# Three ready-made u tiles a head instead of two, turned in halves of 1024 columns over three buffer pairs

## The chip, the cores and the metric

The kernel runs on one core of one Trainium2 chip, in one launch. The metric is the device time of the launch in microseconds (us); lower is better.

## The reference

One decoder layer on 512 tokens of width 2048, in float32:

```
P = rms(x) @ w_in                       # 2048 x 6144: q | k | v | B | C | xc, 1024 columns each
a = 8 heads of differential attention   # softmax(s1) - lam * softmax(s2), applied to v, then rms
c = B * causal_conv3(C * xc)
x = x + concat(a, c) @ w_out
h = rms(x);  for 8 PEER heads: scores of 2 x 128 keys, top 16 of 16 x 16 sums, softmax gates
x = x + sum over the chosen experts e of gelu(h . u[e]) * gate * v[e]      # u, v: 16384 x 2048
```

## The kernel before

**Order of the work.** Five stages follow each other. (1) The qkv stage multiplies h by the first 3072 columns of w_in, in 6 chunks of 512 columns. (2) The heads stage has 8 rounds; each does one attention head and one 128-column block of the short convolution (three products called conv 0, 1 and 2, their weights in six pieces of 8 x 128 x 128 a head). (3) The out stage multiplies by w_out in 4 chunks. (4) The sweep: for 384 of the 512 tokens the product with u is dense over all 128 tiles of u (128 experts each, 16 tiles a sweep, 8 sweeps); the first 128 tokens gather their u and v rows by index. (5) The dense stage multiplies gelu times gate by all of v for 256 tokens and gathers v rows for 128.

Each float32 operand of a matmul is split into a high and a low part: ACT copies the high part (`wc_hi`, `uT_hi`), DVE subtracts it to get the low part (`wc_lo`, `uT_lo`), and PE makes three matmuls (lines L1811 to L1813).

**Queues.** Each engine has an order written out by hand and stops at the first wait that isn't met: SP issues loads on the hardware queue q1, POOL issues stores, zeroing and indirect transfers on the software queue q0, ACT has q10. POOL also computes the inverse roots (L752).

**u tiles.** The sweep needs u transposed. An even tile c is loaded to `u_tile[0]` from u, and PE transposes it with 16 transposes (L2063), 8 after each half of the 48 matmuls of tile c-1; ACT and DVE then split it out of PSUM (L1124, L1654). Of the odd tiles the first 56 (`TURNED`) are ready-made: in stages 1 to 3 SP loads the 128 rows into `near_rows` or `far_rows` (L473), DVE transposes 32 x 32 blocks (L1302, four of 128x512 a tile) into `near_turned` or `far_turned`, and the tile is stored in `uT_all` in DRAM by four transfers, one for each quarter of the partitions (L459). In the sweep SP loads such a tile into `u_tile[1]` (L654) and ACT and DVE split it straight from there (L1119, L1649). `turned_before(tile)` says which tiles these are: odd and below 112.

**A head of stage 2.** Two such tiles are made in each of the first seven heads, in the near pair. SP waits for `wc_ready` of piece p and then loads the piece after next (L566, 512 KB); after pieces 2 and 5 it also loads the next rows (`next_rows`). DVE transposes one tile in two halves among the softmax steps of query blocks 0 to 2, and the other after `o_n` (L1455) and before `qk_n` (L1379). POOL stores the first before it makes the inverse root of `o_ss`, the second after that of `qk_ss`. At the start of the stage DVE makes `wc_lo` of piece 2 and only then the norm of q and k of head 0:

```
            keep_qkv(chunks - 1)
            turn_rows(NEAR, NEAR_HEADS, "qkv")
            split_wc(0, 2)
            ...
            norm_qk(0, 0)
            norm_qk(0, 1)
```

ACT's order in a head, from `split_wc(j, 5)` on, is `exps(3)`, `split_wc(j + 1, 0)`, `keep_aT(2)`, `b_sb`, `split_wc(j + 1, 1)`, `keep_aT(3)`; PE needs aT of block 3 for its last product with v (`apply_v(3)`, L1910).

Of the kernel before, what the change touches and what calls it, by code (L numbers as in the profile page):

```python
# [34 lines left out]
P = 128  # L35
SEQ = 512
D = 2048
# [39 lines left out]
KEPT_BY_POOL = 1 + 2 * (HEADS - 1)  # L77
# [4 lines left out]
TURNED = NEAR_TURNED + FAR_TURNED  # L82
ZERO_DMAS = 2 * HEADS
# [22 lines left out]
def turned_before(tile):  # L106

    return tile % 2 == 1 and tile < 2 * TURNED
# [33 lines left out]
def decoder_layer(nc, x, attn_norm_g, w_in, q_norm_g, k_norm_g, lambda_q1, lambda_k1, lambda_q2, lambda_k2,  # L142
                  subln_g, conv_w, w_out, ffn_norm_g, peer_w_q, peer_subkeys, peer_u, peer_v, out):
    ctx = ExitStack()
    with ctx:
# [111 lines left out]
        seg_turned = [nc.alloc_sbuf_tensor_at("near_turned", [P, QUADS, KT, QUAD], F32, offset=late + 8 * KB), far_turned]  # L257
        wo0_hi = nc.alloc_sbuf_tensor_at("wo0_hi", [P, QUARTER, CHUNK], F32R, offset=late)
# [81 lines left out]
        uT_rows = u_tile[1][:, :].rearrange("p (a k e) -> p k a e", a=QUADS, e=QUAD)  # L340
# [12 lines left out]
        head_mean = sem("head_mean")  # L353
        head_rstd = sem("head_rstd")
# [17 lines left out]
        conv_gated = sem("conv_gated")  # L372
        conv_out = sem("conv_out")
# [43 lines left out]
        seg_kept = sem("seg_kept")  # L417
# [34 lines left out]
        def kept_at(pair, n):  # L452
            return n + pair * NEAR_TURNED

        def store_turned(engine, pair, n, stored):

            rows = uT_all[bass.ds(kept_at(pair, n) * P, P), :].rearrange("(r d) (a m) -> a d r m", r=QUADS, a=QUADS)
            for a in range(QUADS):
                engine.dma_start(rows[a], seg_turned[pair][QUAD * a:QUAD * (a + 1), :, :, :].rearrange("d r k e -> d r (k e)"))\  # L459
                    .then_inc(stored, 16)  # L460


        @nc_block.sync
        def _(sp):
# [7 lines left out]
            def load_rows(pair, n):  # L472
                sp.dma_start(seg_rows[pair][:, :], u_table[bass.ds((2 * kept_at(pair, n) + 1) * P, P), :])\  # L473
                    .then_inc(seg_in[pair], 16)

            def next_rows(pair, n):

                sp.wait_ge(seg_ready[pair], 4 * n + 4)
                load_rows(pair, n + 1)

            def keep_turned(pair, n, last=False):

                sp.wait_ge(seg_ready[pair], 4 * n + 4)
                if not last:
                    load_rows(pair, n + 1)
                store_turned(sp, pair, n, seg_stored[pair])
# [5 lines left out]
            def load_qkv_weights():  # L492

                def chunk(c, first=False):
                    load_wi(c, 0)
                    if first:
                        sp.wait_ge(hT_ps, TB)
                        load_rows(FAR, 0)
                    else:
                        keep_turned(FAR, 2 * c - 1)  # L500
                    load_wi(c, 1)
                    keep_turned(NEAR, 3 * c)
# [1649 lines left out]
```

## Time and profile before

| | us |
|---|---|
| median of 3 runs (2961.92 to 2970.81) | 2964.81 |
| the profiled execution's own time | 2968.59 |
| its span, first to last instruction | 2966.8 |
| qkv stage, heads stage, out stage and routing (about) | 45 to 288, 288 to 625, 625 to 860 |
| sweep, dense stage (about) | 860 to 2210, 2210 to 2960 |
| one head, PE's period | 40.9 |

In the windows view a line gives a stretch, its length, then for PE, the weight loads of PE (PEld), DVE, ACT and POOL the busy us and the count of instructions, the clock that PE was granted (1.00 is full speed), the mean busy share of the 16 DMA engines, and GB/s. In the timeline a line gives start us, length us, engine, line, operation, and in brackets how long the engine had been idle and what ended that. In a row of transfers the last number is the median us from issue to landing.

### The profile page before, as it was taken

To read this page: it belongs to the slowest core of one execution; us is meant where nothing else is said; L and a number is where in the kernel's file an instruction comes from. 1 tells how busy PE (TensorE), PEld (TensorE's weight loads), DVE (VectorE), ACT (ScalarE), POOL (GpSimd) and SP (SyncE) were. 2 spreads that over 40 slices of the span, in tenths; PEclk is the share of its full clock that TensorE was granted. 3 is DMA by queue.
4 is the path that set the end of the run, shared out by engine and by line. 5 is a ranking of instruction groups with operands and counts; after the bars stand their busy time and mean duration, and the time that the engine had idled before them with its cause. 6 is when DMAs were issued, how large, how long until landed. Compare 5 with 4: busy or idle time off the path is not lost.

```text
span 2966.8 us, 40581 instructions
## 1 busy us (share of the span) xinstructions
PE 2889.4 (97%) x14993; PEld 2570.9 (87%) x14993; DVE 2358.4 (79%) x3050; ACT 1048.8 (35%) x1373; POOL 1517.4 (51%) x906
## 2 busy tenths in 40 slices
PE   7999999999999999999999999999999999899898
PEld 6888777888889999999999999999998787777787
DVE  6455677754688888988888898899778898898898
ACT  4122443341323333434333343334233333333333
POOL 1000232300015656665665666566858887778662
PEclk9999999999999999999999999999999999999999
DMA  8998777779658998999899899999999999999998
GB/s 298 332 352 273 254 237 251 227 290 328 229 184 306 323 337 300 341 322 330 308 324 336 301 340 321 330 345 357 325 369 392 415 414 414 414 415 415 415 413 347
DMA packets 333295, 980.65 MB, mean 331 GB/s; under 512 B 63764, under 2 KB 180512, under 8 KB 241760
## 3 DMA queue, kind: packets, MB, share of 16 engines
q1 hardware_dynamic: 188560, 508.60, 46.7%
q0 software_dynamic: 107008, 439.75, 41.2%
q10 hardware_dynamic: 37584, 30.43, 3.2%
q8 instruction: 86, 1.41, 0.2%
q14 instruction: 57, 0.47, 0.0%
HBM read 866.33 MB, written 112.33 MB: 330 GB/s over the span
## 4 chain that ended last, share of the span: by engine, by line
PE 69%; DVE 10%; DMA 9%; issue 5%; POOL 4%; ACT 2%; SPq 0%; ACTq 0%; DVEq 0%; POOLq 0%
PE ps L1811 22%; PE ps L1813 21%; PE ps L1812 21%; DMA v_raw<-in_peer_v 7%; PE ps L2063 3%; DVE x_rows L1669 2%; DVE v_lo L1709 2%; DVE u_row L1660 2%; POOL gate_grid L820 1%; ACT v_hi L1180 1%; POOL dots L828 1%; POOL v_ring L839 1%; DMA gates_of<-gate_grid 1%; PE ps L1894 1%; PE ps L1910 1%
## 5 line engine op out<-in xcount | busy, mean ns | idle before, releaser
L1811 PE MATMUL ps<-hT_hi,uT_hi 128*128 128x384 f32 x2048 | 699.0, 341 | 10.3 <-DVE uT_lo L1649 6.1
L1813 PE MATMUL ps<-h2T_lo,uT_hi 128*128 128x384 f32 x2048 | 686.1, 335 | 0.0
L1812 PE MATMUL ps<-hT_hi,uT_lo 128*128 128x384 f32 x2048 | 685.0, 334 | 0.0
L820 POOL DMA_INDIRECT gate_grid<-gates,grid_cells x256 | 540.7, 2112 | 107.5 <-issue 78.8
L1811 PE MATMUL ps<-v_hi,a_hi 128*128 128x512 f32 x1024 | 404.2, 395 | 38.4 <-DVE v_lo L1709 37.7
L1180 ACT ACTIVATE v_hi<-v_raw 128x2048 fp32r<-128x2048 f32 x128 | 245.6, 1919 | 455.5 <-PE ps L1813 336.1
L1812 PE MATMUL ps<-v_hi,a_lo 128*128 128x512 f32 x1024 | 401.5, 392 | 0.0
L1813 PE MATMUL ps<-v_lo,a_hi 128*128 128x512 f32 x1024 | 401.2, 392 | 0.0
L1811 PEld LDWEIGHTS ps<-hT_hi,uT_hi 128*128 128x128 f32 x2048 | 384.8, 188 | 19.0 <-DVE uT_lo L1649 10.0
L1812 PEld LDWEIGHTS ps<-hT_hi,uT_lo 128*128 128x128 f32 x2048 | 385.0, 188 | 1.9
L1813 PEld LDWEIGHTS ps<-h2T_lo,uT_hi 128*128 128x128 f32 x2048 | 384.3, 188 | 0.0
L839 POOL DMA_INDIRECT v_ring<-in_peer_v,experts x128 | 286.3, 2237 | 136.2 <-DVE x_one L1759 104.8
L1709 DVE TENSOR_TENSOR v_lo<-v_raw,v_hi 128x2048 fp32r<-128x2048 f32 x128 | 293.1, 2290 | 71.7 <-ACT v_hi L1180 67.8
L1759 DVE SCALAR_TENSOR_TENSOR x_one<-v_ring,acts,x_one 128x2048 f32<-128x2048 f32 x128 | 300.3, 2346 | 7.8 <-DMA v_ring<-in_peer_v,experts 5.0
L810 POOL DMA_INDIRECT v_row<-in_peer_v,experts x128 | 140.3, 1096 | 322.7 <-DVE x_rows L1669 273.3
L1669 DVE SCALAR_TENSOR_TENSOR x_rows<-v_row,acts,x_rows 128x2048 f32<-128x2048 f32 x128 | 300.0, 2344 | 1.4 <-issue 1.4
L1660 DVE CUSTOM_DVE_ANT_0 u_row<-u_row,h_rows 128x2048 f32<-128x2048 f32 x128 | 292.6, 2286 | 3.5 <-DMA u_row<-in_peer_u,experts 3.5
L828 POOL DMA_INDIRECT dots<-products_one,cells x128 | 264.9, 2070 | 42.7 <-issue 38.7
L1811 PEld LDWEIGHTS ps<-v_hi,a_hi 128*128 128x128 f32 x1024 | 194.1, 190 | 87.4 <-issue 35.0
L1124 ACT ACTIVATE uT_hi<-ps 128x1024 fp32r<-128x1024 f32 x144 | 148.0, 1028 | 311.4 <-PE ps L2063 287.2
L1654 DVE TENSOR_TENSOR uT_lo<-ps,uT_hi 128x1024 fp32r<-128x1024 f32 x144 | 176.1, 1223 | 101.9 <-ACT uT_hi L1124 99.3
L1811 PE MATMUL ps<-w_hi,hT_hi 128*128 128x512 f32 x624 | 244.1, 391 | 1.2 <-DVE wi_lo L1256 1.2
(207 smaller groups left out, 4970.8 us busy)
## 6 DMA issues: line engine op xcount, KB each, us to landing
v_raw<-in_peer_v SPq DMA_DIRECT2D x128, 1024.0 KB
u_tile<-in_peer_u SPq DMA_DIRECT2D x72, 1024.0 KB
u_tile<-uT_all SPq DMA_DIRECT2D x56, 1024.0 KB
near_rows<-in_peer_u SPq DMA_DIRECT2D x40, 1024.0 KB, 8.4
uT_all<-near_turned SPq DMA_DIRECT2D x100, 256.0 KB, 7.0
w_raw<-in_w_in SPq DMA_DIRECT2D x24, 1024.0 KB, 9.0
wc_raw<-in_w_in SPq DMA_DIRECT2D x48, 512.0 KB, 6.7
far_rows<-in_peer_u SPq DMA_DIRECT2D x16, 1024.0 KB, 9.2
```

Of the source, the lines that this page charges most:

```text
L820: pool.indirect_dma_start(out=gate_grid, out_offset=bass.IndirectOffsetOnAxis(ap=grid_cells[:, d, col:col + 1], axis=0), in_=gates[:, 2 + ...
L828: pool.indirect_dma_start(out=dots[:, s:s + 1], out_offset=None, in_=products_one, in_offset=bass.IndirectOffsetOnAxis(ap=cells[:, col:col ...
L839: pool.indirect_dma_start(out=v_ring[s % RING][:, :], out_offset=None, in_=v_table, in_offset=slot(1, h, s)).then_inc(v_in[s % RING], 16)
L1180: nc.scalar.activation(v_hi[b % 2][:, :], v_raw[b % RAW_RING][:, :], ACT.Copy).then_inc(v_hi_ready, 1)
L1654: v.tensor_tensor(uT_lo[half][:, :, :], ps_uT[half], uT_hi[half][:, :, :].bitcast(F32), ALU.subtract)\
L1660: v.tensor_tensor_reduce(out=u_row[c % 2][:, :], in0=u_row[c % 2][:, :], in1=h_rows[:, 0, :], scale=1.0, scalar=0.0, op0=ALU.mult, op1=ALU ...
L1669: v.scalar_tensor_tensor(out=x_rows[:, 0, :], in0=v_row[c % 2][:, :], scalar=acts0[:, b:b + 1], in1=x_rows[:, 0, :], op0=ALU.mult, op1=ALU ...
L1709: v.tensor_tensor(v_lo[b % 2][:, :], v_raw[b % RAW_RING][:, :], v_hi[b % 2][:, :].bitcast(F32), ALU.subtract).then_inc(v_lo_ready, 1)
L1759: v.scalar_tensor_tensor(out=x_one[:, :], in0=v_ring[s % RING][:, :], scalar=acts[:, s:s + 1], in1=x_one[:, :], op0=ALU.mult, op1=ALU.add) ...
L1811: mm(out, a_hi, b_hi, start=first, stop=False)
L1812: mm(out, a_lo, b_hi, start=False, stop=False)
L1813: return mm(out, a_hi, b_lo, start=False, stop=last)
```

## The change

A head of the first seven now makes three tiles: the two odd ones as before, and the tile at place 6 of the sweep of the same number (tiles 6, 22, ..., 102), so that 63 tiles are ready-made, 7 of them even. The two pairs of stage 2 become three pairs of half buffers: LEFT and RIGHT are the halves of the near pair, THIRD lies at 124 KB and 140 KB of the arena, where `wi_lo` and `far_turned` lie in the qkv stage. Every half tile (128 rows x 1024 columns) is loaded by one 512 KB transfer with rows of 4 KB, transposed by two DVE instructions, and stored by four POOL transfers in runs of 1 KB (before: 1 MB with rows of 8 KB, four instructions, runs of 2 KB). DVE's six places in a head are: after `alibi` and `conv_taps`; after `combined(0)`; after `combined(1)`; after `combined(3)`; and two after `o_n`. SP loads half 0 after piece 1, halves 1 and 2 after piece 2, halves 3, 4 and 5 after pieces 3, 4 and 5. Before the loop of heads SP waits for the end of the qkv matmuls (`proj_done`), because THIRD lies over a buffer that they read; pieces 2 and later of head 0 are behind this wait. In the sweep tile 8 of each of the first seven sweeps is loaded when DVE has split tile 6, not when PE has turned it. Five semaphores are merged into others.

```diff
-KEPT_BY_POOL = 1 + 2 * (HEADS - 1)
+EXTRA = HEADS - 1
+EXTRA_AT = 6
+KEPT_BY_POOL = 1 + 3 * (HEADS - 1)
...
 def turned_before(tile):
 
-    return tile % 2 == 1 and tile < 2 * TURNED
+    if tile % TOPK == EXTRA_AT:
+        return tile // TOPK < EXTRA
+    return tile % 2 == 1 and tile < 2 * ODD_TURNED
...
+        half_rows.append(at("half_rows2", 124, [P, D // HALVES]))
...
+        half_turned.append(at("half_turned2", 140, [P, QUADS, KT // HALVES, QUAD]))
...
+        def half_place(j, i):
+
+            place = extra(j) if i >= 4 else odd_of_head(j, 1 + i // 2)
+            return place, i % 2
+
+        def half_of_head(i):
+
+            return (THIRD, LEFT, RIGHT)[i % 3]
+
+        def halves_turned(j, i):
+
+            return 4 * (NEAR_HEADS + 1) + 2 * (6 * j + i)
...
+            def next_half(j, i):
+
+                (tile, _), half = half_place(j, i)
+                sp.wait_ge(seg_ready[NEAR], halves_turned(j, i) - 4)
+                load_half(half_of_head(i), tile, half)
...
-            for n in range(2):
-                keep_turned(NEAR, NEAR_QKV + n)
+            keep_turned(NEAR, NEAR_QKV, odd(NEAR, NEAR_QKV), odd(NEAR, NEAR_QKV + 1))
+            sp.wait_ge(seg_ready[NEAR], 4 * NEAR_HEADS)
+            for x in (LEFT, RIGHT):
+                load_half(x, odd_of_head(0, 0)[0], x)
+            store_turned(sp, NEAR, odd(NEAR, NEAR_QKV + 1)[1], seg_stored[NEAR])
+            for t in range(TB):
+                sp.wait_ge(proj_done[t], QKV_CHUNKS)
             with sp.Fori(0, CT - 1) as j:
                 for p in range(PIECES):
                     sp.wait_ge(wc_ready, PIECES * j + p + 1)
                     conv_piece(j + (p + 2) // PIECES, (p + 2) % PIECES)
-                    if p in (2, 5):
-                        next_rows(NEAR, 2 * j + (NEAR_HEADS + p // 5))
+                    for i in ((), (0,), (1, 2), (3,), (4,), (5,))[p]:
+                        next_half(j, i)
...
+            def store_half(x, row, half):
+
+                rows = uT_all[bass.ds(row * P, P), :].rearrange("(r d) (a h m) -> a h d r m", r=QUADS, a=QUADS, h=HALVES)
+                for a in range(QUADS):
+                    pool.dma_start(rows[a][half], half_turned[x][QUAD * a:QUAD * (a + 1), :, :, :].rearrange("d r k e -> d r (k e)"))\
+                        .then_inc(half_kept[x], 16)
...
                 if j < HEADS - 1:
-                    keep_turned(NEAR_HEADS + 1 + 2 * j)
-                pool.wait_ge(head_mean, 2 * j + 2)
-                inverse_root(o_ss[:, :]).then_inc(head_rstd, 1)
+                    for i in range(4):
+                        keep_half(j, i)
+                pool.wait_ge(mean_ready, TB + 2 * j + 2)
+                inverse_root(o_ss[:, :]).then_inc(rstd_ready, 1)
...
+            def turn_half(x):
+
+                for q in range(2):
+                    v.transpose(half_turned[x][:, :, 4 * q:4 * q + 4, :].rearrange("p r k e -> p k r e"),
+                                half_rows[x][:, q * CHUNK:(q + 1) * CHUNK]
+                                .rearrange("p (k r d) -> p k r d", r=QUADS, d=QUAD))\
+                        .then_inc(seg_ready[NEAR], 1)
...
+            def turn_half_of_head(j, i):
+
+                x, use = half_of_head(i), 2 * j + i // 3
+                dve.wait_ge(half_in[x], 16 * (HALF_LOADS[x] + use) + 16)
+                dve.wait_ge(half_kept[x], 16 * QUADS * (HALF_STORES[x] + use))
+                turn_half(x)
...
-            turn_rows(NEAR, NEAR_HEADS, "qkv")
+            dve.wait_ge(seg_stored[NEAR], 16 * QUADS * NEAR_HEADS)
+            dve.wait_ge(seg_stored[FAR], 16 * QUADS * FAR_QKV)
+            for x in (LEFT, RIGHT):
+                dve.wait_ge(half_in[x], 16 * HALF_LOADS[x])
+                turn_half(x)
             split_wc(0, 2)
```

## Rows read from the trace of the kernel before

**Rows 1.** The page: busy time of each engine.

```profile
PE 2889.4 (97%) x14993; PEld 2570.9 (87%) x14993; DVE 2358.4 (79%) x3050; ACT 1048.8 (35%) x1373; POOL 1517.4 (51%) x906
```

**Rows 2.** Windows: one head, sweep 1, sweep 6, dense stage.

```profile
385.00:426.00 41.00, 41.00 (x204) 32.50 (x202) 30.53 (x66) 16.11 (x32) 11.67 (x14) 1.00 0.77 245
...
1084.00:1276.00 192.00, 191.13 (x1122) 185.22 (x1121) 163.87 (x254) 70.16 (x112) 123.09 (x73) 1.00 0.94 328
...
1850.00:2045.00 195.00, 192.15 (x1147) 187.96 (x1146) 177.29 (x275) 76.05 (x123) 125.96 (x80) 1.00 0.97 342
...
2250.00:2950.00 700.00, 664.85 (x2878) 543.90 (x2877) 630.44 (x373) 260.79 (x179) 523.12 (x238) 0.99 1.01 410
```

**Rows 3.** Timeline of PE in sweep 0, around the first transposes of tile 6.

```profile
912.66 0.33 PE L1811 MATMUL ps<-hT_hi,uT_hi 128*128 128x384 f32 x1
...
915.61 0.34 PE L1813 MATMUL ps<-h2T_lo,uT_hi 128*128 128x384 f32 x1
915.78 1.03 PE L2063 MATMUL ps<-ident,u_tile 128*128 128x128 f32 x8
...
916.83 0.34 PE L1812 MATMUL ps<-hT_hi,uT_lo 128*128 128x384 f32 x1
```

**Rows 4.** Waits of the sweep: us in total, times, longest.

```profile
PE ps L1811 <- DVE uT_lo L1649: 4.8, 7, 1.3
```

**Rows 5.** Chain that ended last, at the end of the sweep.

```profile
2200.50 0.69 DVE dots_at L1714
```

**Rows 6.** Timeline of DVE in one head.

```profile
389.34 1.31 DVE L1302 STREAM_TRANSPOSE near_turned<-near_rows 128x512 f32<-128x512 f32 x2 [0.40 <-DMA near_rows<-in_peer_u]
...
406.98 1.23 DVE L1270 TENSOR_TENSOR wc_lo<-wc_raw,wc_hi 128x1024 fp32r<-128x1024 f32 x1 [2.29 <-ACT wc_hi L915]
...
426.99 0.29 DVE L1405 CUSTOM_DVE_ANT_0 probs<-ps,alibi 128x128 f32<-128x128 f32 x1 [1.77 <-PE ps L1894]
```

**Rows 7.** Timeline of ACT in the same head.

```profile
405.89 1.06 ACT L915 ACTIVATE wc_hi<-wc_raw 128x1024 fp32r<-128x1024 f32 x1 [3.15 <-DMA wc_raw<-in_w_in]
406.85 0.58 ACT L972 ACTIVATE aT<-ps 128x512 f32<-128x512 f32 x1
```

**Rows 8.** Timeline of PE in the same head, at apply_v(3).

```profile
408.18 1.05 PE L1910 MATMUL ps<-qkv,aT 128*128 x8
```

**Rows 9.** Timeline of POOL in the same head.

```profile
395.81 2.20 POOL L459 DMA_DIRECT2D uT_all<-near_turned  x4 [10.93 <-DVE near_turned L1302]
410.87 1.46 POOL L752 TENSOR_TENSOR o_ss<-o_ss,minus_half 128x4 f32<-128x4 f32 x1 [12.86 <-DVE o_ss L1450]
```

**Rows 10.** Transfers of pieces issued at 383.6, 391.9 and 402.0.

```profile
wc_raw<-in_w_in SPq DMA_DIRECT2D x1, 512.0 KB, 13.0
...
wc_raw<-in_w_in SPq DMA_DIRECT2D x1, 512.0 KB, 6.1
...
wc_raw<-in_w_in SPq DMA_DIRECT2D x1, 512.0 KB, 3.8
```

**Rows 11.** DMA, 385 to 405 in 40 slices of 0.5 us.

```profile
GB/s 369 386 344 410 407 394 398 412 412 382 414 410 418 373 415 407 375 364 372 346 315 200 156 160 239 246 115 221 188 352 328 221 188 8 0 0 122 254 287 412
```

**Rows 12.** DMA queue of ACT's stores, 900 to 2000: packets, MB, share of 16 engines.

```profile
q10 hardware_dynamic: 29545, 20.17, 6.0%
```

**Rows 13.** Timelines of DVE, ACT and PE where the heads stage begins.

```profile
288.90 0.69 DVE L1265 COPY qkv<-ps 128x512 f32<-128x512 f32 x1 [4.75 <-PE ps L1813]
...
290.73 1.06 ACT L915 ACTIVATE wc_hi<-wc_raw 128x1024 fp32r<-128x1024 f32 x1 [3.96 <-DMA wc_raw<-in_w_in]
...
298.81 1.29 DVE L1379 TENSOR_TENSOR qk_n<-qkv,qk_ss 128x512 f32<-128x512 f32 x2 [3.05 <-POOL qk_ss L752]
...
299.57 1.24 PE L1926 MATMUL ps<-ident,qk_n 128*128 128x128 f32 x8
```

**Rows 14.** Tile 8 of sweep 0: SP's load, PE's first transposes.

```profile
921.89 0.33 SPq L654 DMA_DIRECT2D u_tile<-in_peer_u  x1
...
939.76 1.03 PE L2063 MATMUL ps<-ident,u_tile 128*128 128x128 f32 x8
```

More of the change, by code:

```diff
@@ L82 @@
 TURNED = NEAR_TURNED + FAR_TURNED
+ODD_TURNED = TURNED - EXTRA
+HALVES = 2
+HEAD_MEANS = 2 * HEADS
+LEFT, RIGHT, THIRD = 0, 1, 2
+HALF_USES = 2 * (HEADS - 1)
+HALF_LOADS = (NEAR_QKV + 3, FAR_QKV + 1, 0)
+HALF_STORES = (1, 1, 0)
+NEAR_STORES = NEAR_TURNED - KEPT_BY_POOL
 ZERO_DMAS = 2 * HEADS
@@ L449, in decoder_layer, with odd, odd_of_head, extra @@
         nc_block = ctx.enter_context(nc.Block())
[L452 to L457, printed above, removed]
+        def odd(pair, n):
+            k = n + pair * (NEAR_TURNED - EXTRA)
+            return 2 * k + 1, k
+        def odd_of_head(j, m):
+            k = NEAR_HEADS + 2 * j + m
+            return 2 * k + 1, k
+        def extra(j):
+            return TOPK * j + EXTRA_AT, ODD_TURNED + j
+        def store_turned(engine, pair, row, stored):
+            rows = uT_all[bass.ds(row * P, P), :].rearrange("(r d) (a m) -> a d r m", r=QUADS, a=QUADS)
             for a in range(QUADS):
@@ L492, in load_qkv_weights, with keep_odd @@
             def load_qkv_weights():
+                def keep_odd(pair, n, last=False):
+                    keep_turned(pair, n, odd(pair, n), None if last else odd(pair, n + 1))
                 def chunk(c, first=False):
@@ L528, in far, with keep_odd @@
                     return FAR_QKV + 2 * c
+                def keep_odd(pair, n, last=False):
+                    seen = EXTRA if pair == NEAR else 0
+                    keep_turned(pair, n, odd(pair, n - seen), None if last else odd(pair, n - seen + 1))
                 for q in range(1, 4):
@@ L559, in _ @@
             load_quarter(w_in_v, 0, 1, range(4))
-            load_rows(NEAR, 0)
+            load_rows(NEAR, odd(NEAR, 0)[0])
             load_qkv_weights()
@@ L1292, in turn_rows @@
                 if parts[0] == 0:
-                    dve.wait_ge(seg_in[pair], 16 * n + 16)
+                    if stage == "qkv":
+                        loads, stores = n, n
+                    elif pair == NEAR:
+                        loads, stores = n - NEAR_OUT + HALF_LOADS[LEFT] + HALF_USES, n - KEPT_BY_POOL
+                    else:
+                        loads, stores = n + 1 + HALF_USES, n
+                    dve.wait_ge(seg_in[pair], 16 * loads + 16)
                     if isinstance(n, int) and n == 0:
                         pass
-                    elif stage == "heads":
-                        dve.wait_ge(seg_kept, 16 * QUADS * (n - NEAR_HEADS))
-                    else:
-                        by_pool = KEPT_BY_POOL if (pair, stage) == (NEAR, "out") else 0
-                        dve.wait_ge(seg_stored[pair], 16 * QUADS * (n - by_pool))
+                    else:
+                        dve.wait_ge(seg_stored[pair], 16 * QUADS * stores)
                 for q in parts:
@@ L1396, in head @@
                                    vec[:, V_CONV:N_VEC].rearrange("p (a c) -> p a c", a=TAPS)[:, :, bass.ds(j, 1)]))
+                if not last:
+                    turn_half_of_head(j, 0)
                 def biased(qb):
@@ L1428, in head @@
                 if not last:
-                    turn_rows(NEAR, 2 * j + (NEAR_HEADS + 1), "heads", range(2))
+                    turn_half_of_head(j, 1)
                 split_wc(j, 4)
@@ L1433, in head @@
                 if not last:
-                    turn_rows(NEAR, 2 * j + (NEAR_HEADS + 1), "heads", range(2, 4))
+                    turn_half_of_head(j, 2)
                 biased(3)
@@ L1443, in head @@
                 if not last:
+                    turn_half_of_head(j, 3)
                     split_wc(j + 1, 1)
@@ L1503, in rest_of_chunk @@
                 split_wo(c + 1, 1)
-                turn_rows(NEAR, 3 * c + NEAR_OUT, "heads" if first else "out")
+                if first:
+                    for x in (LEFT, RIGHT):
+                        dve.wait_ge(half_kept[x], 16 * QUADS * (HALF_STORES[x] + HALF_USES))
+                turn_rows(NEAR, 3 * c + NEAR_OUT, "out")
             split_wo(0, 3)
```

145 lines of the change are left out of this document (78 added, 67 removed).

## The prediction

> **What bounds the kernel now.** I read the page first: PE is busy 97% of the span, DVE 79%, ACT and POOL half or less [rows 1]. So the first question is whether PE is the bound in each stage that the change touches, and the windows by stage answer it [rows 2]. In a head PE is busy all of 41 us, DVE 30.5, POOL 11.7, and the DMA engines 77%. In sweep 1 PE is busy 191.1 of 192 us, DVE 163.9, DMA 94%. In sweep 6, which has no queries to multiply, DVE is busy 177.3 of 195 and PE loses 2.9 us. The dense stage is another case: 665 of 700 us of PE, but the DMA engines are at 1.01 and 410 GB/s all the way, so its length is that of its transfers, counted from where it starts. What comes before it moves it as a whole.
>
> Next, the waits of the sweep. The longest sums belong to ACT and POOL, which wait for PE; of PE itself only 4.8 us are lost to a late `uT_lo` [rows 4]. Then the chain of waits at the end of the sweep: it goes through POOL's scatters and the load of their result to the first product on DVE at 2200.5 [rows 5], while PE starts the dense stage at about 2211. That chain begins with the last head's choices, which are made in sweep 6, before the last sweep. It moves with PE; it is no fixed floor. The reader should keep two things: the sweep is where PE time can be removed and shows in full, and the heads stage is PE-bound with DMA and DVE close behind, with less room than shares of busy time suggest.
>
> **The change, part by part.**
>
> *PE's transposes in the sweep.* PE starts a matmul of 384 columns every (915.61 - 912.66) / 17 = 0.174 us. From the last one before the transposes to the second after them it takes 916.83 - 915.61 = 1.22 us, where two steps are 0.35: eight transposes cost 0.87 us [rows 3]. A tile has two such groups, 1.74 us. Seven tiles less: 12.2 us. Six of them are followed or preceded by a quarter of the queries (2.8 us of PE), which hides the split of the second half of tile 6, as it does for its odd neighbours. In sweep 6 there is no such cover and DVE has only 195 - 177.3 = 17.7 us idle over 16 tiles, 1.1 a tile [rows 2]. There I take half the 1.74 us as lost, 0.9 (from 0 to 1.7). DVE's and ACT's own work for a ready-made tile is as long as for one out of PSUM, so nothing is added there. **Sum: -12.2 + 0.9 = -11.3 us.**
>
> *Tile 8's load* now waits for DVE's split of tile 6 instead of PE's transposes. It was issued at 921.89 and first used at 939.76, 17.9 us later [rows 14]. The split ends some 3 to 4 us after the transposes, and PE gets there 1.7 us sooner, so 12 to 13 us are left; the odd tiles live with about 14 between heads with queries and 10 to 12 without, and wait for none. Cost nothing; were it late, a tile would pay the difference, at most a few us in all.
>
> *The start of the heads stage.* Here something is lost once. SP now waits for the end of the qkv matmuls, which releases the last copy at 288.90, before it loads pieces 2 and later. ACT had piece 2 at 290.73, DVE then made its low part, and behind that in DVE's order stands the whole norm of head 0. `qk_n` starts at 298.81, its first half ends at about 299.5, and PE takes it at 299.57 with no idle time before [rows 13]. So the slack is 0 to 0.1 us, and whatever delays piece 2 delays PE. Issued at about 289.2 into queues that are then nearly empty, a piece lands in 3.8 us, the time of the one issued at 402 [rows 10]: 293.0 instead of 290.7. **+2.2 us**; below, 1.5 if it lands sooner; above, the 13.0 us of the piece issued into the fullest queue would make it 11, but the two half loads ahead have landed by then, so I take 6 as the upper bound.
>
> *DVE in a head.* Two more half tiles are transposed, each of two instructions as in 1.31 us [rows 6]: 2.6 us, of 41 - 30.5 = 10.5 idle [rows 2]. Where they stand matters. Half 0 comes before the scores of block 0, where DVE is idle for 1.77 us; half 3 comes before `wc_lo` of piece 1, where it is idle for 2.29 us [rows 6]. The other four stand where the two tiles stood. Both gaps are longer than 1.31 us, so DVE costs nothing; without that cover it would be 2.6 us a head.
>
> *POOL in a head.* Four stores take 2.20 us to issue. They were 8 a head and are 24: +8.8 us on 11.7 busy. Half 3's stores stand before the inverse root of `o_ss`. DVE turns half 3 at about 404.7 to 406.0, the stores take until 408.2, and the inverse root starts at 410.87 [rows 9]: 2.7 us of slack, against such issues of 0.55 us each [rows 9]. The last two halves end before POOL waits for the convolution's output. Nothing.
>
> *DMA in a head.* This is the part that I trust least. A head moves 1 MB more in and 1 MB more out, 12 MB instead of 10 in 40.9 us. The added load at 400 GB/s (the plateau in the slices, [rows 11]) is 2.6 us. Stores out of one quarter of the partitions ran at about 200 GB/s (the slices from 395 to 401), which makes the third tile 5 us. No row shows them in 1 KB runs: below, they are no slower per byte; above, they take as long per run as 2 KB ones, and three tiles cost 30 us where two cost 10. I take a value near the low end, because the nearest rows are ACT's stores in the sweep, half of 512 B and half of 1 KB: 29545 packets in 6.0% of 16 x 1100 us, 36 ns for 683 B on average [rows 12], so short runs need not be slow. So 0.77 of 41 us, 31.6, becomes about 39: full, but not over. What counts is where. The stretch in which POOL zeroes cells, to 394, runs at the plateau, and it is there that the piece issued at 383.6 takes 13.0 us [rows 10]. Spare room follows from 395 to 401.5, and an idle us [rows 11]. Into these 7 us, of which some 3 are free, go the stores of half 0 (2.4), the load of half 3 (1.3) and that of half 4 (1.3), 5.0 us. About 2 us are left over at 402, when the piece is issued that ACT has been waiting for: it lands at 405.89 [rows 7] after the shortest time of all, 3.8 us. Behind it in ACT's order is aT of block 3, ready at 406.85 + 0.58 = 407.43, which PE needs at 408.18 [rows 8]: 0.75 us of slack. If it shares the engines with 2 us of other work, it lands 1 to 2 us later, and PE waits 0.2 to 0.7 us; each us of waiting also gives the engines room, which damps it. I take 0.4 us a head, seven heads: **+2.8 us** (0 to 7 without saturation). The piece issued at 391.9 lands after 6.1 us [rows 10], at 398.0, and is needed at about 401.8; it comes out at the same size.
>
> On this the Trainium skill, DMA: Bandwidth & Descriptors, section Queues, rings and completion order, says that each DMA engine goes round between the queues it has work for, a packet at a time. The trace agrees: the 13.0 us piece is on SP's queue while POOL's zeroing is on the other. By that rule small packets lose to large ones, and 1 KB runs of POOL hold a piece up less than the zeroing does; it speaks for the low end.
>
> *All.* -11.3 + 2.2 + 2.8 = **-6.3 us**. The profiled execution took 2968.6 us, so it would take 2962.3; it was 3.8 above the median of the runs, and from the median it is 2958.5. I predict **2958.5 us**.
>
> **Rivals.**
>
> (a) *No stall in the heads.* Damping and packet order hide the 2 us. For it: every gap that the six halves use is longer than they are, and sum of bytes over plateau is only 30 us of 41. Against: the 0.75 us of slack. Then -11.3 + 2.2 = -9.1: 2955.7; with the start costing 1.5 and sweep 6 giving all, -10.7: 2954.1.
>
> (b) *The heads become DMA-bound: the other side.* Place: ACT's wait for pieces 0 and 1 of the next head. Price: if the 1 KB runs cost what the 2 KB runs do, the third tile and the splitting of the other two add 20 us and the load 2.6 to 31.6, 54 us in a head of 41. Any value between is possible. Each us a head costs 7; from 9.1 / 7 = 1.3 us a head the kernel is no faster, and from (9.1 + 8.9) / 7 = 2.6 us it is slower by over 0.3%. At 2 us: +4.9, 2969.7. Against: ACT's short stores [rows 12]. The Trainium skill has a rule on the same page, section Bandwidth, that takes this rival's side: batch transfers to 1 MiB or more for three quarters of the peak, where halves have 512 KB. That a piece of 512 KB alone takes 3.8 us [rows 10] agrees with a fixed part, but the plateau shows such parts overlapped [rows 11].
>
> (c) *The sweep doesn't give it back.* DVE, not PE, sets the pace in stretches, and what PE gains at tile 6 it waits for later as `uT_lo`. Then -11.3 becomes about -4 and the sum +1: 2966. For it: DVE's 17.7 us in sweep 6. Against: 28 us idle in sweep 1 [rows 2], and 4.8 us of such waits in all [rows 4].
>
> (d) *One late load of tile 8 a sweep*, 1 us each: 2965.
>
> **How the numbers follow.** The forecast 0.45, with its own range from 2955.7 (nothing lost in the heads) to 2962.7 (7 us lost); (a) 0.29; (b) 0.13; (c) 0.09; (d) 0.04. A measurement can tell about 0.3%, 8.9 us, from no change: 2955.9 to 2973.7 is no change. Of (a), most lies just below 2955.9, the cases where the start costs more above it: 0.2 of the 0.29; from the forecast's low edge and unknown gains 0.07. Faster 0.27. Slower needs 2.6 us a head: half of (b), 0.06 with what I have overlooked. Same 0.67. The range: from 2952.5, (a) with a start that costs nothing (-11.3 is 2953.5) and a us for noise, up to 2967, which takes in (c), (d) and (b) up to 1.6 us a head.
>
> **What would show it.** In the sweep, PE has 1040 transposes of u instead of 1152, and passes 5 to 6 of each of the first seven sweeps are 1.7 us shorter; the end of the last sweep against the end of the heads comes 11 us earlier. `qk_n` of head 0 starts at about 301 and PE stands idle 2 us before it. A head's period is 41.3 instead of 40.9; if it is 40.9, (a) holds, if over 42, (b). ACT's wait for `wc_raw` in heads grows from 3.15 us. The DMA share in heads is above 0.9. PE's waits for `uT_lo` beyond 10 us in the sweep would be (c). The prediction is wrong if stores in 1 KB runs cost as much each as 2 KB ones, or if the late piece 2 delays more than PE's first transposes.

## The result, and the profile after

The kernel after takes 2973.47 us (median of 20 runs, 2967.48 to 2977.51), the one before 2967.41 (20 runs beside it): a ratio of 1.002, interval 1.0014 to 1.0027. So it is 4 to 8 us slower, which is real and less than 0.3%; I had forecast 2958.5. Of the 15.0 us between the two, 2.6 lie in the base: the forecast started from a median of 2964.81 us in 3 runs of before, which is 2967.41 in 20. The profiled execution has a span of 2971.9 us where that of before had 2966.8. One execution counts in none of the times below, the profiled one of experiment 8, which took 3923.56 us at a mean clock of 0.68 and therefore gives no periods either.

The page and the windows of after, to be read beside [rows 1] and [rows 2]:

```profile
PE 2884.3 (97%) x14881; PEld 2562.4 (86%) x14881; DVE 2375.2 (80%) x3078; ACT 1049.8 (35%) x1373; POOL 1568.9 (53%) x1022
```

```profile
core 0: us, PE busy (x) PEld busy (x) DVE busy (x) ACT busy (x) POOL busy (x), PEclk, DMA share, GB/s
385.00:426.00 41.00, 39.30 (x194) 30.76 (x193) 31.08 (x68) 15.77 (x32) 18.30 (x27) 1.00 0.85 284
...
1084.00:1276.00 192.00, 191.02 (x1109) 184.75 (x1108) 168.91 (x258) 73.95 (x117) 122.58 (x73) 1.00 0.94 327
1850.00:2045.00 195.00, 191.28 (x1135) 186.66 (x1134) 177.04 (x273) 75.53 (x122) 123.14 (x79) 1.00 0.96 339
2250.00:2950.00 700.00, 668.65 (x2883) 547.09 (x2882) 629.09 (x374) 261.56 (x181) 521.57 (x241) 0.98 1.01 411
```

PE has 112 instructions fewer, seven tiles of 16 transposes. The loss shows in one row: in a head PE is no longer busy all the time, 39.3 of 41 us, although the mean DMA share is only 0.85.

The quickest way to split the span is by a mark that stands in both kernels, here the start of PE's transposes of `qk_n`, one a head (L1926 in [rows 13], L2034 after):

| us | before | after | difference |
|---|---|---|---|
| head 0 starts | 299.57 | 303.03 | +3.5 |
| from there to head 7, seven heads | 286.50 | 300.13 | +13.6 |
| from head 7 to the end | 2380.7 | 2368.7 | -12.0 |
| span | 2966.8 | 2971.9 | +5.1 |

The single heads of after last 41.1, 42.5, 43.1, 42.5, 45.0, 42.1 and 43.9 us; before, 41.1 and then 40.9. What PE waits for, in the timeline of PE of after:

```profile
303.03 1.26 PE L2034 MATMUL ps<-ident,qk_n 128*128 128x128 f32 x8 [3.01 <-DVE qk_n L1480]
...
369.74 0.66 PE L2011 MATMUL ps<-ident,probs 128*128 128x128 f32 x4 [1.36 <-DVE probs L1524]
...
412.82 0.66 PE L2011 MATMUL ps<-ident,probs 128*128 128x128 f32 x4 [1.64 <-DVE probs L1524]
...
496.11 0.94 PE L2018 MATMUL ps<-qkv,aT 128*128 x6 [0.38 <-ACT aT L1051]
498.68 0.66 PE L2011 MATMUL ps<-ident,probs 128*128 128x128 f32 x4 [1.64 <-DVE probs L1524]
```

In six of the seven heads it is the same place, and 8.6 of the 9.8 us of idle time in these heads belong to it (the other 1.2 us are two waits for `aT`): the transposes of the probabilities of query block 3, which are late on DVE. To see why, follow the head that starts at 386.62 back through its queues. The timelines of DVE, of ACT and of SP's queue, of after:

```profile
409.86 1.22 DVE L1349 TENSOR_TENSOR wc_lo<-wc_raw,wc_hi 128x1024 fp32r<-128x1024 f32 x1 [2.97 <-ACT wc_hi L994]
411.00 0.16 DVE L1520 RECIPROCAL inv_sum<-row_sum 128x2 f32<-128x2 f32 x1
...
412.02 0.75 DVE L1524 SCALAR_TENSOR_TENSOR probs<-probs,inv_sum 128x512 f32<-128x512 f32 x1
```

```profile
408.76 1.06 ACT L994 ACTIVATE wc_hi<-wc_raw 128x1024 fp32r<-128x1024 f32 x1 [2.57 <-DMA wc_raw<-in_w_in]
409.73 0.47 ACT L1051 ACTIVATE aT<-ps 128x384 f32<-128x384 f32 x1
...
412.32 1.06 ACT L994 ACTIVATE wc_hi<-wc_raw 128x1024 fp32r<-128x1024 f32 x1 [1.64 <-DMA wc_raw<-in_w_in]
413.51 0.60 ACT L1051 ACTIVATE aT<-ps 128x512 f32<-128x512 f32 x1
```

```profile
388.64 0.38 SPq L624 DMA_DIRECT2D wc_raw<-in_w_in  x1
391.05 0.33 SPq L524 DMA_DIRECT2D half_rows<-in_peer_u  x1
396.44 0.38 SPq L624 DMA_DIRECT2D wc_raw<-in_w_in  x1
397.16 3.57 SPq L524 DMA_DIRECT2D half_rows<-in_peer_u  x1
407.05 0.38 SPq L624 DMA_DIRECT2D wc_raw<-in_w_in  x1
```

The first four of these five loads land as follows; each row is the answer for a stretch of 0.3 us around the issue, and its last number is the us to landing:

```profile
wc_raw<-in_w_in SPq DMA_DIRECT2D x1, 512.0 KB, 15.1
half_rows<-in_peer_u SPq DMA_DIRECT2D x1, 512.0 KB, 14.2
wc_raw<-in_w_in SPq DMA_DIRECT2D x1, 512.0 KB, 12.3
...
half_rows<-in_peer_u SPq DMA_DIRECT2D x1, 512.0 KB, 13.2
```

The piece issued at 396.44 is piece 0 of the next head. Before, it took 6.1 us [rows 10]; now it takes 12.3 and lands at 408.74. ACT's copy follows at once, then DVE's low part at 409.86, and only behind that, in DVE's written order, the softmax of block 3, which ends at 412.77; PE starts at 412.82. New in SP's queue ahead of that piece is half 3's load, issued at 391.05, 3.5 us after POOL issued its zeroing. From 388.64 to 408.74 the DMA share is 1.01: the mean of 0.85 over a head hides a full stretch.

### The profile page after: what moved, and what is told of

Its sections match the earlier page's. It is cut to its first block, busy times and chain, and to the rows that moved or that the text cites. A ratio compares the mean times of both kernels' runs of the same rounds, so it can differ in the third digit from the quotient of the medians.

```text
span 2971.9 us, 40688 instructions
## 1 busy us (share of the span) xinstructions
PE 2884.3 (97%) x14881; PEld 2562.4 (86%) x14881; DVE 2375.2 (80%) x3078; ACT 1049.8 (35%) x1373; POOL 1568.9 (53%) x1022
## 4 chain that ended last, share of the span: by engine, by line
PE 62%; DVE 17%; DMA 12%; issue 5%; ACT 3%; DVEq 0%; ACTq 0%; SPq 0%; POOL 0%
PE ps L1919 19%; PE ps L1921 19%; PE ps L1920 19%; DMA v_raw<-in_peer_v 9%; DVE x_rows L1777 3%; PE ps L2171 3%; DMA wc_raw<-in_w_in 3%; DVE u_row L1768 3%; DVE v_lo L1817 2%; ACT v_hi L1259 1%; DVE uT_lo L1762 1%; DVE uT_lo L1757 1%; DVE x_one L1867 1%; DVE half_turned L1392 1%; DMA w_raw<-in_w_in 1%
## 5 line engine op out<-in xcount | busy, mean ns | idle before, releaser
L898 POOL DMA_INDIRECT gate_grid<-gates,grid_cells x256 | 534.0, 2086 | 107.3 <-issue 78.9
L1919 PEld LDWEIGHTS ps<-hT_hi,uT_hi 128*128 128x128 f32 x2048 | 384.7, 188 | 21.2 <-DVE uT_lo L1757 17.0
L888 POOL DMA_INDIRECT v_row<-in_peer_v,experts x128 | 147.3, 1151 | 319.3 <-DVE x_rows L1777 274.5
L1777 DVE SCALAR_TENSOR_TENSOR x_rows<-v_row,acts,x_rows 128x2048 f32<-128x2048 f32 x128 | 300.1, 2344 | 1.3 <-ACT acts L1212 1.3
L837 POOL DMA_DIRECT2D uT_all<-half_turned x176 | 96.3, 554 | 385.2 <-DVE half_turned L1392 382.6
L1920 PE MATMUL ps<-w_hi,hT_lo 128*128 128x512 f32 x624 | 243.3, 390 | 0.0
```

The source lines that it names most:

```text
L888: pool.indirect_dma_start(out=v_row[b % 2][:, :], out_offset=None, in_=v_table, in_offset=slot(0, i, b)).then_inc(v0_in[b % 2], 16)
L898: pool.indirect_dma_start(out=gate_grid, out_offset=bass.IndirectOffsetOnAxis(ap=grid_cells[:, d, col:col + 1], axis=0), in_=gates[:, 2 + ...
L1777: v.scalar_tensor_tensor(out=x_rows[:, 0, :], in0=v_row[c % 2][:, :], scalar=acts0[:, b:b + 1], in1=x_rows[:, 0, :], op0=ALU.mult, op1=ALU ...
L1919: mm(out, a_hi, b_hi, start=first, stop=False)
L1920: mm(out, a_lo, b_hi, start=False, stop=False)
```

## The experiments

All times are medians beside runs of the kernel before on the same chip, 2966.5 to 2967.4 us in all of them; there is no number 7. Heads are counted from 0, so the seven periods are those of heads 0 to 6. The table gives the start of head 0 and the seven periods from the profile of each.

| kernel | us | ratio to before, interval | head 0 starts | seven heads |
|---|---|---|---|---|
| before | 2967.41 | | 299.57 | 41.1, then 40.9 |
| after | 2973.47 | 1.0014 to 1.0027 | 303.03 | 41.1, 42.5, 43.1, 42.5, 45.0, 42.1, 43.9 |
| 1 sweep only | 2955.43 | 0.9957 to 0.998 | 299.55 | 41.1, then 40.9 |
| 2 wait moved | 2969.49 | 1.0003 to 1.0022 | 301.07 | 41.2, 46.2, 42.3, 43.1, 42.2, 42.5, 42.5 |
| 3 zeroing spread | 2959.55 | 0.9967 to 0.9987 | 302.24 | 42.7, then 40.9 |
| 4 two tiles in halves | 2978.49 | 1.0032 to 1.0066 | 301.98 | 42.7, 42.6, 42.6, 40.9, 42.7, 43.3, 41.1 |
| 5 half 3 behind | 2961.01 | 0.9969 to 0.9988 | 301.73 | 42.4, 41.1, 40.9, 41.2, 41.0, 40.9, 40.9 |
| 6 softmax first | 2959.37 | 0.9964 to 0.9984 | 301.96 | 42.6, then 40.9 |
| 8 start, zeroing | 2957.69 | 0.9957 to 0.9979 | not shown | not shown |
| 9 two, half 3 behind | 2971.67 | 1.0003 to 1.0022 | 302.78 | 42.4, 40.9 five times, 43.3 |
| 10 start, softmax first | 2954.92 | 0.9945 to 0.9971 | 301.31 | 41.2, then 40.9 |
| 11 all three | 2956.88 | 0.9965 to 0.9985 | 299.74 | 41.2, then 40.9 |

**1. The sweep's part alone, on the kernel before.** It leaves out the making of the seven tiles: in their place it loads rows that hold another tile, so its output is wrong and only its time is of use.

```diff
-    return tile % 2 == 1 and tile < 2 * TURNED
+    return tile % 2 == 1 and tile < 2 * TURNED or tile % TOPK == 6 and tile < 2 * TURNED
...
```

> The kernel before, with tiles 6, 22, ..., 102 loaded as ready-made ones from rows that hold another tile: only the sweep's part of the change, with wrong values for these seven tiles, and with nothing added to the heads. Theory 'the sweep gives 12 us and the heads take more than that back': 2967.4 - 12 = 2955 us (between -11 and -12.5), heads still 40.9 us. Rival 'DVE sets the sweep's pace': 2961 or more, with PE's waits for the low part of u well above the 10 us of the kernel before.

Measured: 11.6 us below the before of its call, heads untouched. The gain in the sweep is there, and in full: -12.0 in the profile of after too, where my sum had -11.3.

**2. The wait for the qkv matmuls moved behind pieces 2 and 3 of head 0.**

```diff
-            for t in range(TB):
-                sp.wait_ge(proj_done[t], QKV_CHUNKS)
...
+            def head_loads(j, first=False):
...
+                    if first and p == 1:
+                        for t in range(TB):
+                            sp.wait_ge(proj_done[t], QKV_CHUNKS)
...
```

> The changed kernel with the wait for the end of the qkv matmuls moved behind the loads of pieces 2 and 3 of head 0, in front of the first load into the third buffer. If that wait alone delays the first norm of q and k: PE's transposes of head 0 start at about 299.6 to 300 instead of 303.0, and the time falls by 3.5 us to 2970. If the delay came from the two half loads or from POOL's eight stores: no change, 2973.5. The heads' periods stay at 42 to 45 us either way.

Measured: the start comes at 301.07, 2.0 us of the 3.5 back, not all. The pieces now stand behind the store of what the texts call tile 17 (row 17 of `uT_all`, the last ready-made tile of the qkv stage), whose four issues take SP 3.7 us; piece 2 is issued at 284.78 and lands after 7.5 us. The seven heads take 299.9 us, as in after: the start and the heads are separate losses.

**3. The zeroing spread.** POOL zeroes one block of cells after each of its two inverse roots, instead of both at the head's start.

```diff
-                for n in range(2 * j, 2 * j + 2):
-                    zero_cells(n)
...
                 inverse_root(o_ss[:, :]).then_inc(rstd_ready, 1)
+                zero_cells(2 * j)
...
                     inverse_root(qk_ss[:, :]).then_inc(rstd_ready, 1)
+                zero_cells(2 * j + 1)
...
```

> The changed kernel with POOL's two 1 MB transfers that zero the gate grid moved from the start of a head to behind the two inverse roots, where the DMA engines were idle; the same bytes in all. Theory 'a burst at the start of a head delays the piece that the next head starts with, and the split of that piece blocks the softmax on DVE': the period of a head falls from 42.9 to 41 to 41.5 us and the time by 10 to 13 us, to 2961 to 2964. Theory 'the engines are full over the whole head': the period stays at 42.5 or more, the time within 3 us of 2973.5.

Measured: the heads lose nothing any more (40.9 in six of seven; the 42.7 of head 0 is taken up in the last section), and the time is 1.5 us below the range that I had expected. All 12 MB a head are still moved: the DMA share in the window 385 to 426 is 0.91, higher than in after. Piece 0 of the next head, issued at 396.76, lands after 6.5 us instead of 12.3. Over a whole head there is bandwidth enough; what matters is when the transfers run.

**4. Two tiles a head as before, but in halves over three buffers.** The third tile is left out, half 3's load stays where after has it.

```diff
-EXTRA = HEADS - 1
+EXTRA = 0
...
-                    for i in ((), (0,), (1, 2), (3,), (4,), (5,))[p]:
+                    for i in ((), (0,), (1, 2), (3,), (), ())[p]:
...
```

> Two tiles a head as before, but moved in halves over the three buffer pairs; no extra tile, PE turns tile 6 in every sweep. Theory 'the bytes of the third tile are what the heads can't hide': the period is 40.9 to 41.1, only the 3.5 us at the start remain, 2967.4 + 3.5 = 2971. Rival 'halving is what costs' (twice as many stores, issued by POOL, in short runs): the period stays at 42 or more, 2967.4 + 3.5 + 8 = 2979 or more.

Measured: five of the seven heads are as late as in after, or nearly, with the bytes of before (DMA share 0.75 and 237 GB/s over 300 to 588, before 0.76 and 240); the seven take 295.9 us, where before has 286.5 and after 300.1. My theory that the third tile's bytes cost the time fell here, and the time is the one that I had given to its rival, that halving the transfers costs; 5 and 9 test that. The new suspect is half 3's load, in front of piece 0. The loads of this kernel around there (issued at 389.42, 391.88 and 397.27) land as those of after do:

```profile
wc_raw<-in_w_in SPq DMA_DIRECT2D x1, 512.0 KB, 14.3
half_rows<-in_peer_u SPq DMA_DIRECT2D x1, 512.0 KB, 13.4
wc_raw<-in_w_in SPq DMA_DIRECT2D x1, 512.0 KB, 11.6
```

**5. Half 3's load behind piece 0 of the next head,** all three tiles made.

```diff
-                    for i in ((), (0,), (1, 2), (3,), (4,), (5,))[p]:
+                    for i in ((), (0,), (1, 2), (), (3, 4), (5,))[p]:
```

> The changed kernel with the load of half 3 moved from behind piece 5 to behind the next head's piece 0, so that this piece has 512 KB less in front of it in SP's queue. Theory 'the load of half 3 ahead of the piece is what delays it': the piece lands 2 to 3 us sooner than the 12.3 us after its issue, PE's waits for the probabilities of block 3 end, periods of 41 to 41.5 us, about 2963. Rival 'POOL's zeroing and stores take the engines, whatever SP's order': the piece still takes over 9 us, or half 3 becomes the late one; periods of 42 or more, 2971 to 2975.

Measured: of the six heads that were late in after, four are back at 40.9 to within 0.1 us, two at 41.1 and 41.2. Piece 0, issued at 395.07, lands after 9.2 us: 3.1 us sooner than in after, and still 3.1 us later than in before. So half 3's load in front is half of the lateness, and without it the rest fits into the slack. The rival's sign, a landing over 9 us, came true, its periods didn't. One transfer of 512 KB moved by one place in SP's order is worth some 12 us.

**6. The softmax of block 3 before the split of pieces 0 and 1,** loads as in after.

```diff
 ACT:
                 exps(3)
-                if not last:
-                    split_wc(j + 1, 0)
-                else:
+                if last:
...
-                if not last:
-                    split_wc(j + 1, 1)
-                else:
+                if last:
                     split_mix(0)
                 keep_aT(3)
+                if not last:
+                    split_wc(j + 1, 0)
+                    split_wc(j + 1, 1)
...
 DVE:
                 split_wc(j, 5)
-                if not last:
-                    split_wc(j + 1, 0)
-                else:
+                if last:
                     split_wo(0, 0)
                 combined(3)
                 if not last:
                     turn_half_of_head(j, 3)
+                    split_wc(j + 1, 0)
                     split_wc(j + 1, 1)
...
```

> The changed kernel with the same transfers, but ACT and DVE split the next head's pieces 0 and 1 only after the softmax of block 3 (and, on ACT, after the last copy of aT), so that a late piece stops nothing of this head. Theory 'the DMA burst costs time only because the split of a late piece stands ahead of the softmax in DVE's and ACT's order': periods of 40.9 to 41.2, the 3.5 us at the start remain, 2967 + 3.5 - 12 = 2959. Theory 'the DMA engines are full over the head': the wait moves to conv 0 of the next head, periods of 42 or more, 2972.

Measured: 40.9 in six of seven heads, and yet the piece lands as late as in after. The timeline of DVE, and the piece's row of the transfers (issued at 395.28):

```profile
404.51 1.22 DVE L1348 TENSOR_TENSOR wc_lo<-wc_raw,wc_hi 128x1024 fp32r<-128x1024 f32 x1
405.65 0.16 DVE L1519 RECIPROCAL inv_sum<-row_sum 128x2 f32<-128x2 f32 x1
...
406.67 0.75 DVE L1523 SCALAR_TENSOR_TENSOR probs<-probs,inv_sum 128x512 f32<-128x512 f32 x1
...
411.76 1.22 DVE L1348 TENSOR_TENSOR wc_lo<-wc_raw,wc_hi 128x1024 fp32r<-128x1024 f32 x1 [3.12 <-ACT wc_hi L994]
```

```profile
wc_raw<-in_w_in SPq DMA_DIRECT2D x1, 512.0 KB, 12.4
```

The same wait of 3 us on DVE is there, but nothing that PE needs soon stands behind it. So both halves of the cause are shown: the late transfer (3, 5) and the order that lets it hold up the softmax (6). Taking away either is enough. The edit moves the splits on ACT and on DVE together; that DVE's order carries most of the loss is read from PE's waits in after, 8.6 us for `probs` against 1.2 for `aT`.

**9. As 4, with half 3's load behind piece 0,** to test the place at equal bytes.

```diff
-                    for i in ((), (0,), (1, 2), (3,), (), ())[p]:
+                    for i in ((), (0,), (1, 2), (), (3,), ())[p]:
...
```

> Two tiles a head in halves, with the load of half 3 behind the next head's piece 0; the bytes of a head are those of the kernel before. Theory 'with equal bytes only the place of that load delays the piece': periods of 40.9, 2971 (the start's 3.5 us). Rival 'stores of half tiles right behind the zeroing delay it': periods of 42 or more, 2976 or more.

Measured: five heads at 40.9, 6.8 us less than 4, so halving itself costs nothing there. The last still loses 2.4 us, at the same wait for block 3's probabilities: its piece 0 lands 12.4 us after its issue, where in the five others it takes 8.4 to 9.4. Why it does in that head is open. The profiled execution is one of the two slowest of this kernel (2976.31 us).

**8, 10 and 11. Combinations.** All three issue piece 2 of head 0 right behind the two half loads, ahead of the store of tile 17 and of the wait for the qkv matmuls:

```diff
...
+            sp.wait_ge(wc_ready, 1)
+            conv_piece(0, 2)
             store_turned(sp, NEAR, odd(NEAR, NEAR_QKV + 1)[1], seg_stored[NEAR])
...
```

8 has the spread zeroing with it, 10 the order of 6, and 11 both.

> The changed kernel with the zeroing spread as in the run that gave 40.9 us a head, and with piece 2 of head 0 issued before the last store of the qkv stage and before the wait for its matmuls. If the start costs what its delay costs, and the drop of the clock after PE's idle 2.8 us goes with it: PE's transposes of head 0 at 299.6 to 300, all periods 40.9 to 41.1, 2959.5 - 3 to - 4.5 = 2955 to 2956.5, 12 us below the kernel before. If something else delays the first norm, 2959.

> The order of e6 (ACT and DVE split pieces 0 and 1 of the next head only after the softmax of query block 3), and at the start of the heads stage piece 2 of head 0 issued right behind the two half loads, ahead of the store of tile 17 and of the wait for the qkv matmuls. Theory (start and heads are separate losses, both now avoided): PE starts the transposes of head 0 at 299.6 to 300.5, with less than 1 us idle before it, the period of head 0 is 40.9 to 41.2 (the 42.6 of e6 came from the granted clock that fell to half after the idle 2.2 us, and goes with it), the six after it are 40.89, and the time is 4 us below that of e6: some 2955 to 2956. Rival 1 (the 42.6 of head 0 has another cause, such as a late piece): the start gets better by 2 us, the period of head 0 stays at 42 or more, 2957 to 2958. Rival 2 (the early issue only moves the wait, as the first move of the wait did): start at 301 or later, 2959.

> As e10, and the zeroing of the cells spread behind the two inverse roots. If the two ways of sparing the heads are alternatives (each alone gave 40.89 in six of seven heads, with nothing left to gain), it takes the time of e10 within 2 us: 2955 to 2957. If one of them makes room that the other still needs, it is more than 2 us faster; if the later zeroing now holds up the load of piece 0 or 1 of the next head, more than 2 us slower, with periods above 41. Start at 299.6 to 300.5 as in e10.

Measured: 2957.69, 2954.92 and 2956.88 us, of which 10 is 11.6 us below before and the fastest version of the study. 8 missed its range, 2955 to 2956.5, and lies between it and the 2959 of its rival; without periods it decides nothing. In 10 the start is at 301.31, not the 300.5 at most that I expected, yet the 42.6 us of head 0 are 41.2: that part of the theory holds. In 11 the start is as before:

```profile
299.74 1.26 PE L2042 MATMUL ps<-ident,qk_n 128*128 128x128 f32 x8 [0.40 <-DVE qk_n L1489]
```

The two kernels have the same code there. What differs is when DVE may transpose the two halves of the first ready-made tile of the heads stage, which waits for the store of tile 17: in 10 it is idle 1.50 us for that, in 11 0.48. The store stands behind the early piece 2 in SP's order; SP comes to it 1.3 us sooner in 11. Half a us of the difference lies further ahead, in the qkv stage, whose last copy comes at 289.05 in 10 and at 288.50 in 11. Why these executions differ is open, so the start of 11, as early as before, is not shown to be due to its edit. 10 and 11 differ by 2 us, and their intervals overlap; the second remedy for the heads adds nothing to the first.

## Why the prediction was wrong

**The step that failed is the heads term, +2.8 us; it measured +13.6.** Of the two pieces I followed one and let the other go with "it comes out at the same size". That is the one: it lands 5.7 us later in its head. I put the loss at ACT's copy of piece 1, with 0.75 us of slack in front of aT of block 3; piece 1 did land later, 5.2 us after its issue instead of 3.8, but PE waits for aT of block 3 nowhere in the heads of after. The trace of before had the numbers for piece 0 too. I read its need at about 401.8, where DVE's low part starts; these lines of ACT and of DVE, of before, show what stands behind it:

```profile
400.68 1.04 ACT L915 ACTIVATE wc_hi<-wc_raw 128x1024 fp32r<-128x1024 f32 x1
```

```profile
400.65 2.35 DVE L1270 TENSOR_TENSOR wc_lo<-wc_raw,wc_hi 128x1024 fp32r<-128x1024 f32 x2
...
403.94 0.75 DVE L1421 SCALAR_TENSOR_TENSOR probs<-probs,inv_sum 128x512 f32<-128x512 f32 x1
```

ACT took the piece 2.6 us after it had landed at 398.07, and DVE ended the softmax at 404.69, 1.0 us before PE took it at 405.68: 3.6 us of slack. The piece was issued at 391.9, where the zeroing held the plateau. I weighed the bytes added after 395; half 3's load is issued at +4.4 us in the head, before that, into the same queue as piece 0 and ahead of it. Its neighbour in that stretch, piece 5, took 13.0 us already [rows 10]. With such a landing in front of it piece 0 could not keep 6.1. From 388.64 to 408.74, when it lands, the engines move 7.24 MB, where in before from 383.6 to 398.0 they had moved 5.08.

The slack can be held against every head. In before piece 0 lands at 16.5 us into the head that starts at 381.61; with 3.6 us of slack it may land at 20.1. Counted like this, for heads 1 to 6 of each profile:

| kernel | piece 0 lands, us into the head | periods |
|---|---|---|
| before | 16.1 to 16.5 | 40.9 |
| after | 21.5, 22.1, 21.5, 22.4, 21.2, 22.9 | 42.5, 43.1, 42.5, 45.0, 42.1, 43.9 |
| 2 | 23.7, 21.4, 22.1, 21.2, 21.5, 21.5 | 46.2, 42.3, 43.1, 42.2, 42.5, 42.5 |
| 3 | 17.3 to 19.0 | 40.9 |
| 4 | 21.7, 21.6, 19.5, 21.6, 22.3, 20.1 | 42.6, 42.6, 40.9, 42.7, 43.3, 41.1 |
| 5 | 18.3 to 19.4 | 40.9 to 41.2 |
| 6 | 21.2 to 23.5 | 40.9 |
| 9 | 18.3, 18.3, 18.5, 18.5, 19.4, 22.3 | 40.9 five times, 43.3 |

Where the order is that of after, every head whose piece lands later than 20.1 is late, by about as much as the piece is (the 45.0, and the 46.2 of experiment 2, have some 1.6 us of the clock on top, below), and of the others none by more than about 0.3 us. In the order of 6 the same landings cost nothing.

The second half of the miss: I named aT as what stands behind the late piece, on ACT. On DVE the piece's low part stands in front of the whole softmax of block 3, 1.77 us of work, and PE needs that first. Experiment 6 shows that the order of the splits carries the loss.

**The damping did not come.** I let each us of waiting give room back. But the loads and the zeroing follow PE's own progress, so a head that is late starts its transfers late too, and each head loses afresh: in heads 1 to 6 of after the first zeroing is issued 0.9 to 1.0 us and piece 0 9.8 to 9.9 us after the head's start, however late the head before was. This is read from the traces and wasn't tested by itself.

**The clock adds to it.** The idle time of PE in the seven heads sums to 9.8 us, not 13.6. In the head of 45.0 us two idle stretches of 0.38 and 1.64 us lie 2.6 us apart, and what follows is this, in the windows of after:

```profile
499.00:500.00 1.00, 1.00 (x7) 0.86 (x5) 1.00 (x3) 0.60 (x1) 0.00 (x0) 0.70 1.07 319
500.00:501.00 1.00, 1.00 (x4) 0.81 (x3) 0.94 (x1) 0.00 (x0) 0.86 (x2) 0.50 0.28 82
501.00:502.00 1.00, 1.00 (x4) 0.71 (x4) 0.00 (x0) 0.00 (x0) 1.00 (x3) 0.50 0.64 131
502.00:503.00 1.00, 1.00 (x5) 0.81 (x4) 0.00 (x0) 0.00 (x0) 0.31 (x1) 0.59 0.84 145
503.00:504.00 1.00, 1.00 (x10) 0.96 (x10) 0.00 (x0) 0.09 (x1) 0.00 (x0) 1.00 0.75 204
```

The granted clock is at or near 0.50 for over 3 us, that is 1.2 GHz. Two matmuls six steps apart in the timeline of PE of after:

```profile
499.83 0.63 PE L1921 MATMUL ps<-hT_lo,wc_hi 128*128 128x512 f32 x1
...
502.39 0.59 PE L1921 MATMUL ps<-hT_lo,wc_hi 128*128 128x512 f32 x1
```

One starts every (502.39 - 499.83) / 6 = 0.427 us instead of 0.227, and eight of them cost 1.6 us more. The remaining 2 us are no idle time that the timeline names: PE's busy time over the seven heads is 290.25 us where it was 286.50, 3.7 more, in which the 1.6 are contained. What the rest is was not followed up. Nor does such a pair of waits always bring the clock down: in the last of the seven heads PE is idle for 0.82 and 1.63 us, 2.6 us apart, and the clock stays at 1.00.

**The start, +2.2 us; it measured +3.5.** The place was right: `qk_n` is late by piece 2, PE idle 3.01 us. The size was off because the piece took 4.7 us to land, not 3.8, and because the issue of two pieces came at 289.57, not 289.2. ACT's copy came at 294.25, 3.5 us later than in [rows 13]:

```profile
294.25 1.06 ACT L994 ACTIVATE wc_hi<-wc_raw 128x1024 fp32r<-128x1024 f32 x1 [7.19 <-DMA wc_raw<-in_w_in]
```

**What held.** The sweep, -11.3 forecast and -12.0 measured, where seven tiles at 1.74 us are 12.2; experiment 1 gives the same alone. Rival (c) is out, although its sign, over 10 us of waits for `uT_lo` in the sweep, came true. The sign was a poor one: over the whole sweep PE waited 6.1 us at that line in before, more than the 4.8 of [rows 4], and in experiment 1, where the time fell in full, 10.1. Of after, 860 to 2210:

```profile
PE ps L1919 <- DVE uT_lo L1757: 10.5, 17, 1.3
```

Tile 8's load (rival d) shows no wait. POOL's and DVE's added work costs nothing of its own in a head: experiments 3 and 6 do all of it at 40.9 us. Rival (b), the other side, had the right size (2 us a head, 2969.7; measured 1.95 a head, and a period over 42 was its sign) by the wrong mechanism: it asked for short stores that fill the engines, and experiments 3 and 6 move all of these bytes at no loss in heads 1 to 6, 5 at about 0.3 us a head at most. I had given it 0.13; its time deserved more, because the place of a load was a case that I had not made a rival at all.

The Trainium skill, DMA: Bandwidth & Descriptors, section Queues, rings and completion order, has each engine go round between the queues it has work for. I used that rule for the low end, and experiment 3 agrees with it so far as the zeroing goes: with it out of the way the piece lands in 6.5 us instead of 12.3. But inside SP's own queue the loads land in the order of issue in the trace of after (403.7, 405.3, 408.7), and that is what I left out.

## What to carry to other kernels

A load added to a queue can be paid for by the load behind it (here 3.1 us later, 12.3 against 9.2): look up for every transfer behind the new one when it lands, when it is first needed, and what stands behind its user on each engine that has a fixed order, and do it for each, not for the tightest alone. Put an added load behind the next urgent one, and put work on late data behind work that the bottleneck engine waits for; either alone took back all but 1.5 to 1.9 us of the 13.6 that the heads had lost. A mean DMA share of 0.85 says neither that there is room nor that there is none: at 0.91 with the zeroing spread, the same bytes cost nothing, and inside the 0.85 lay 20 us at 1.01.

## What the runs showed of the hardware that I had not expected

**Short idle times of PE can cost more than themselves.** At the start of the heads stage PE is idle for 2.2 to 3.0 us in six profiled executions. In experiment 5, 2.32 us, the windows show this:

```profile
301.00:302.00 1.00, 0.27 (x1) 0.27 (x2) 1.00 (x2) 0.00 (x0) 1.00 (x2) 0.69 0.96 385
302.00:303.00 1.00, 1.00 (x6) 1.00 (x6) 1.00 (x2) 0.12 (x1) 0.69 (x1) 0.50 0.97 385
303.00:304.00 1.00, 1.00 (x6) 0.90 (x5) 0.83 (x3) 0.83 (x2) 0.00 (x0) 0.50 1.04 393
304.00:305.00 1.00, 1.00 (x4) 0.79 (x3) 0.93 (x2) 0.42 (x1) 0.00 (x0) 0.61 0.99 324
```

Experiments 3, 4, 6 and 9 (2.84, 2.58, 2.22 and 3.03 us idle) look the same, each with the clock at 0.50 for a little over 3 us, and head 0 lasts 42.4 to 42.7 us in all five; in the profile of after, with 3.01 us, the clock stayed at 1.00 and the head at 41.1. With 1.70, 1.42 and 0.40 us idle (experiments 2, 10, 11) it stayed at 1.00 as well. So the drop came in five of the six profiled executions with the longer idle time, and costs 1.2 to 1.6 us (42.35 to 42.70 against 41.14). The length of one idle time does not settle it: after, with 3.01 us, shows no drop, and in experiment 2 the head of 46.2 us shows one, at 369.9, where waits of 1.43 and 1.64 us stand 2.6 us apart.

**The issue of a load can itself block.** SP's instruction for 512 KB mostly takes 0.33 to 0.38 us, but 3.57 us at 397.16 in after, when two loads of its queue had been under way for over 6 us, 3.83 at the same place in experiment 6 (395.99), and 2.96 for half 3 in experiment 5 (395.73). SP issued nothing else meanwhile; here its next load came at 407.05, so nothing was lost by it. A caution for reading this: a timeline row of SP's queue with x2 or more runs from the first issue to the last and has SP's waiting between them in it.
